# Attention with V stationary and the turned probabilities split and moving

## The reference, cut to what matters

```python
def one_block(qb):
    s = jnp.einsum('bqhd,bkhd->bhqk', qb, k, preferred_element_type=jnp.float32) * scale
    p = jax.nn.softmax(s, axis=-1)
    return jnp.einsum('bhqk,bkhd->bqhd', p.astype(v.dtype), v)
```

## Time and profile before

| | us |
|---|---|
| median of 3 timed runs | 3041.29 |
| lowest and highest | 3038.35, 3042.91 |
| span of the profiled execution | 3038.7 |
| PE busy in it | 2967.0 (98%) |
| DVE, ACT, POOL busy | 1924.1, 1176.6, 1527.5 |
| first score product to first product of the output projection | 120.5 to 641.1 |

### The profile page before, as it was taken

The page is one execution under the profiler, slowest core; times in us unless marked ns, Lnnn a source line. Parts: engine busy times, 40 slices in busy tenths (PEclk is TensorE's granted clock), DMA queues, the critical chain, the costliest instruction groups (busy, mean ns, idle before and its releaser), DMA issues.

```text
span 3038.7 us, 50018 instructions
## 1 busy us (share of the span) xinstructions
PE 2967.0 (98%) x19166; PEld 2684.5 (88%) x19166; DVE 1924.1 (63%) x2960; ACT 1176.6 (39%) x2027; POOL 1527.5 (50%) x997
## 2 busy tenths in 40 slices
PE   8999999999999999999999999999999999999998
PEld 8999999999999999999999988677777788888776
DVE  6677777755534445777788851677778934445666
ACT  4465666641333334553111122232323533334552
POOL 4100000043777777765444444467674577777774
PEclk9999999999999999999999999999999999999998
DMA  3000100021223334442233423333333232235442
GB/s 128 26 30 27 37 26 16 16 100 49 72 95 99 103 100 163 140 144 71 87 117 94 138 90 118 116 119 101 123 94 118 67 107 102 99 103 171 149 130 90
DMA packets 195934, 286.73 MB, mean 94 GB/s; under 512 B 14709, under 2 KB 105077, under 8 KB 195701
## 3 DMA queue, kind: packets, MB, share of 16 engines
q1 hardware_dynamic: 156096, 236.23, 23.8%
q10 hardware_dynamic: 39605, 47.34, 4.7%
HBM read 208.64 MB, written 74.86 MB: 93 GB/s over the span
## 4 chain that ended last, share of the span: by engine, by line
PE 80%; DVE 7%; POOL 5%; issue 4%; DMA 2%; ACT 1%; SPq 1%; DVEq 0%; ACTq 0%; POOLq 0%
PE PS L1272 72%; PE PS L1528 4%; PE PS L1513 2%; DMA Wraw<-in_w 1%; POOL Wlo L1108 1%; POOL Wlo L1168 1%; PE PS L1872 1%; POOL SQ L1213 1%; SPq L911 0%; DVE GD L3627 0%; POOL RMS L1178 0%; POOL Wraw L1126 0%; POOL Wraw L1124 0%; DVE MX L3007 0%; PE PS L2024 0%
## 5 line engine op out<-in xcount | busy, mean ns | idle before, releaser
L1272 PE MATMUL PS<-Uhi,Whi 128*128 128x352 f32 (+2 forms) x2028 | 512.4, 328 | 16.5 <-DVE Ulo L2799 13.8
L1272 PE MATMUL PS<-Uhi,Wlo 128*128 128x352 f32 (+2 forms) x2028 | 507.3, 326 | 0.0
L1272 PE MATMUL PS<-Ulo,Whi 128*128 128x352 f32 (+2 forms) x2028 | 507.0, 326 | 0.0
L1108 POOL TENSOR_TENSOR Wlo<-Wraw,Whi 128x512 fp32r<-128x512 f32 x242 | 329.8, 1366 | 130.4 <-ACT Whi L2442 127.1
L1272 PEld LDWEIGHTS PS<-Uhi,Whi 128*128 128x128 f32 x2028 | 340.9, 189 | 39.4 <-issue 15.9
L1067 POOL TENSOR_TENSOR Whi<-Wraw,const 128x1024 fp32r<-128x1024 f32 x64 | 159.1, 2486 | 418.4 <-PE PS L1272 403.4
L1272 PEld LDWEIGHTS PS<-Ulo,Whi 128*128 128x128 f32 x2028 | 343.5, 189 | 20.3
L1272 PEld LDWEIGHTS PS<-Uhi,Wlo 128*128 128x128 f32 x2028 | 343.4, 189 | 19.5
L2442 ACT ACTIVATE Whi<-Wraw 128x512 fp32r<-128x512 f32 x242 | 151.3, 629 | 330.7 <-POOL Wraw L1126 133.3
L1156 POOL TENSOR_TENSOR Olo<-H,Ohi 128x1056 fp32r<-128x1056 f32 x5 | 12.1, 2444 | 521.8 <-ACT Ohi L2345 521.8
L1272 PE MATMUL PS<-T,Whi 128*128 128x264 f32 (+1 forms) x1328 | 219.1, 288 | 2.1 <-DVE H L3311 1.9
(11 more groups left out here) (431 smaller groups left out, 7114.4 us busy)
## 6 DMA issues: line engine op xcount, KB each, us to landing
Wraw<-in_w SPq DMA_DIRECT2D x192, 256.0 KB, 3.0
Wraw<-in_w SPq DMA_DIRECT2D x91, 512.0 KB, 3.7
Wraw<-in_w SPq DMA_DIRECT2D x168, 128.0 KB, 2.7
xt<-XTT ACTq DMA_DIRECT2D x20, 640.0 KB, 5.7
opd<-HID SPq DMA_DIRECT2D x40, 264.0 KB, 3.4
T<-opd SPq DMA_DIRECT2D x18, 528.0 KB, 4.3
Ulo<-opd SPq DMA_DIRECT2D x17, 528.0 KB, 4.8
Ulo<-opd SPq DMA_DIRECT2D x17, 512.0 KB, 5.5
```

Source lines behind the costliest of these rows:

```text
L1108: pool.tensor_tensor(f.oplo[j % SLOTS], FIRST_S2 if (p, k) == (0, 6) else f.factors[k], f.ophi[j % SLOTS].bitcast(F32), ALU.subtract).then ...
L1272: ins = pe.matmul(out, lhsT, rhs, start=start, stop=stop, skip_group_check=True)
```

## The change

The output product changes sides. V is stationary, and the turned probabilities move. Both are split: for a head x the tile VH[x % 2] holds in 64 of its 128 columns the highs of V and in the other 64 the lows, so that one pass makes both products, in two halves of the partitions. The turned probabilities of a sequence are collected in PTH (highs) and PTL (lows), [106, 5 key blocks, 528 queries]. A product runs for half a sequence, 264 queries: five key blocks, high and low of the probabilities, ten instructions. The four halves of a head run on PE at the steps 5, 7, 10 and 12 behind the head's first (10 and 12 are n = 0 and 2 of the next head), one step after the step that follows their last operand. The result has features on the partitions. ACT copies the other half of the partitions aside (`other_half`), and DVE adds the two into H (`add_outputs`); both stand one step behind the product. It is not scaled: the sums of a pair are inverted at once (`invert`), transposed, sent through DRAM to all partitions (`save_sums`, `load_sums`) and multiplied in on POOL (`scale_outputs`); for the last pair PE spreads them (`spread_sums`) and DVE multiplies (`scale_last`). `outputs` in float32, `evict`, `take_turned`, `turn_outputs` and `take_outputs_of` go.

The split of the turned probabilities takes all five blocks on ACT (`high_turned`, two instructions a step) and again on DVE (`low_turned`, two). The turn and scaling of queries and keys, all their lows, half of the key highs, the lows of V and of the weights move from DVE and ACT to POOL. The first result of `maximum` goes to an unused column of the score bank in PSUM instead of an SBUF tile.

```diff
+PV_TURNS = {5: (0, 0), 7: (0, 1), 10: (1, 0), 12: (1, 1)}
 # PE, step t
-                if t >= 2:
-                    outputs(t - 2)
+                if half_at_turn(t):
+                    outputs(*half_at_turn(t))
+        def outputs(x, s, h):
+            pe.wait_ge(pt_high, 2 * last_block(x, s, h) + 2)
+            pe.wait_ge(pt_low, 2 * last_block(x, s, h) + 2)
+            pe.wait_ge(v_lo, x + 1)
+            if (x, s, h) != (0, 0, 0):
+                pe.wait_ge(o_evicted, half_number(x, s, h))
+            of = slice(h * QHALF, (h + 1) * QHALF)
             for b in range(KB):
+                low = PTL[b // TURN_FIRST][:, b % TURN_FIRST, of]
+                for i, probs in enumerate((PTH[:, b, of], low)):
+                    ins = mm(PS[:, A_OUT, 0:QHALF], VH[x % 2][:, s * KB + b, :], probs,
+                             start=(b == 0 and i == 0), stop=(b == KB - 1 and i == 1))
 # ACT, step t
-                    take_turned(t - 1)
-                if t >= 0:
-                    exponentials_of(t)
-                if t >= 2:
-                    evict(t - 2)
+                    high_turned(t - 1)
+                exponentials_of(t)
+                if half_at_turn(t, 1):
+                    other_half(*half_at_turn(t, 1))
+                if j and j % 4 == 0 and n == 1:
+                    high_values(j)
                 if nxt < HEADS:
-                    if n == 5:
+                    if n == 3 and nxt % 4:
+                        high_values(nxt)
+                    if n == 6:
                         high_q(nxt)
-                    if n == (1 if nxt % 2 else 6):
+                    if n == 7 and nxt % 2 == 0:
                         high_k(nxt)
 # DVE, step t
-                if t >= 0:
-                    maximum(t)
+                maximum(t)
                 if t >= 1:
-                    take_turned(t - 1)
-                    invert(t - 1)
+                    low_turned(t - 1)
+                if half_at_turn(t, 1):
+                    add_outputs(*half_at_turn(t, 1))
+                if j and j % 2 == 0 and n == 1:
+                    invert(j // 2 - 1)
                 if nxt < HEADS:
                     if nxt % 2 == 0 and n < 2:
                         key_factors(nxt // 2, n)
-                    if n == (0 if nxt % 2 else 5):
-                        scale_keys(nxt)
-                    if n == 4:
-                        turn_queries(nxt)
-                    if n == (7 if nxt % 2 else 6):
-                        low_q(nxt)
-                    if n == (2 if nxt % 2 else 7):
-                        low_k(nxt)
-                    if n in ((6, 9) if nxt % 2 else (8, 9)):
+                    if n in (8, 9):
                         query_factors(nxt, n == 9)
+        def add_outputs(x, s, h):
+            own, n = slice(x % 2 * VD, (x % 2 + 1) * VD), half_number(x, s, h)
+            vec.wait_ge(ob_made, n + 1)
 # POOL, head j
+            if nxt % 2:
+                scale_keys(nxt)
+            if j and j % 4 == 0:
+                low_values(j)
+            if nxt % 2:
+                high_k(nxt)
+                low_k(nxt)
+            if nxt % 4:
+                low_values(nxt)
+            if j % 2 and split_unit(j) is not None:
+                low_weights(j)
+            if j >= 4 and j % 2 == 0:
+                scale_outputs(j // 2 - 2)
+            turn_queries(nxt)
+            if j % 2 == 0 and split_unit(j) is not None:
+                low_weights(j)
+            if nxt % 2 == 0:
+                scale_keys(nxt)
+            low_q(nxt)
+            if nxt % 2 == 0:
+                low_k(nxt)
 # maximum, DVE
-            step(vec.tensor_reduce(MX[:, t % RING:t % RING + 1], PS[0:CW, score_bank(t):score_bank(t) + 2, 0:QHALF], AX_XY, ALU.max))
+            most = PS[0:CW, score_bank(t), QHALF:QHALF + 1]
+            step(vec.tensor_reduce(most, PS[0:CW, score_bank(t):score_bank(t) + 2, 0:QHALF], AX_XY, ALU.max))
```

More of the change, by code:

```diff
@@ L389, in prep_orders @@
             stats.append(("t", nxt // 2))
+        elif j:
+            stats.append(("s", j // 2 - 1))
         stats.append(("q", nxt))
-        if turned_pair(j) is not None:
-            prep += [("o", turned_pair(j), s) for s in both]
         if nxt % 4 == 0:
@@ L407, in score_bank, with half_at_turn, half_number, sums_slot @@
     n = t - (HEADS - 1) * PER_HEAD
-    return A_PREP if n in (1, 3, 5, 7) else A_SCORE
+    return A_PREP if n > 0 and n % 2 else A_SCORE
+PV_TURNS = {5: (0, 0), 7: (0, 1), 10: (1, 0), 12: (1, 1)}
+def half_at_turn(t, late=0):
+    for n, (s, h) in PV_TURNS.items():
+        x, rest = divmod(t - late - n, PER_HEAD)
+        if rest == 0 and 0 <= x < HEADS:
+            return x, s, h
+    return None
+def half_number(x, s, h):
+    return 4 * x + 2 * s + h
+def sums_slot(x):
+    return K_R1SQ if x % 2 else (K_R1, K_RB)[x // 2 % 2]
+def last_block(x, s, h):
+    return x * PER_HEAD + s * KB + (KB - 1 if h else KB // 2)
 def split_unit(j):
@@ new lines, in high_k, with low_k, low_values @@
+        def high_k(x):
+            pool.wait_ge(k_scaled, 2 * x)
+            pool.tensor_tensor(KHI[x % 2][:], KSC[x % 2], one.broadcast_to([P, T]), ALU.mult).then_inc(k_hi, 1)
+        def low_k(x):
+            pool.wait_ge(k_hi, x + 1)
+            pool.tensor_tensor(KLO[x % 2][:], KSC[x % 2], KHI[x % 2][:].bitcast(F32), ALU.subtract).then_inc(k_lo, 1)
+        def low_values(x):
+            own, other_ = (slice(e * VD, (e + 1) * VD) for e in (x % 2, 1 - x % 2))
+            pool.wait_ge(v_hi, x + 1)
+            pool.tensor_tensor(VH[x % 2][:, :, other_], V[:, :, x // 2 % 2, own], VH[x % 2][:, :, own].bitcast(F32),
+                               ALU.subtract).then_inc(v_lo, 1)
@@ L1583, in _ @@
                         query_norms(nxt, n - 4)
-                    o = 4 if nxt % 2 else 6
-                    if turned_pair(j) is not None and o <= n < o + 2:
-                        turn_outputs(turned_pair(j), n - o)
                     if nxt % 4 == 0 and n >= 6:
@@ L1593, in _ @@
                             key_norms((nxt + 1) // 2, n - 8)
-                elif n == 8:
-                    turn_outputs(PAIRS - 1, 0)
         t = HEADS * PER_HEAD
         turn_probs(t - 1)
-        outputs(t - 2)
-        outputs(t - 1)
-        turn_outputs(PAIRS - 1, 1)
+        pe.wait_ge(stats_taken, len(STATS))
+        pe.wait_ge(p_full, t)
+        spread_sums(0)
+        for h in range(2):
+            outputs(HEADS - 1, 1, h)
+        spread_sums(1)
         now["slot"] = None
@@ L2385, in _ @@
         t = HEADS * PER_HEAD
-        take_turned(t - 1)
-        evict(t - 2)
-        evict(t - 1)
-        take_outputs_of(PAIRS - 1, 1)
+        high_turned(t - 1)
+        for h in range(2):
+            other_half(HEADS - 1, 1, h)
         high_out(PAIRS - 1)
```

362 lines of the change are left out of this document (208 added, 154 removed).

## The result

The changed kernel takes 3185.29 us (median of 4 runs, 3174.65 to 3199.14), the one before 3040.72 in the same comparison: 1.0477 of the time, 95% interval 1.0441 to 1.0512. The forecast was 3083 us with a range up to 3112; the sign was right, the size was not: +145 us instead of +42.

The account below looks back on a forecast made before the run. The prediction took a 2.95 us loop through scores, maximum, factor and exponential to bound light steps. Steps +12, POOL +20, ends +5 and clock +5 made +42 us: 3083 us, range 3062 to 3112.

Parts of the forecast that it names:

- a loop of 2.95 us: Attention steps: scores, maximum, factor, exponential, then the next scores into the same PSUM bank; a step costs at least 2.95 us.
- the 2.9 that was to mean a shorter loop: Sign of being wrong: light attention steps under 2.9 us would mean the loop got shorter.
- PE is the bound: Rival: PE's work sets the attention stage's time, so the change gains 92 us, 2949 us; faster in all had chance 0.16.
- The step table: Times of a head's ten steps from PE work, loop and queue delays: four heads 135.5 against 132.5, +12 us over 15.
- the forecast's 4.9 for POOL: Second part of the query factors waits for POOL's key high and low; the next maximum is 4.9 us late.
- +5, between 0 and 20 if light steps n = 8 and 9 suffice: Clock term: the four stalls lower PE's granted clock towards 1.2 GHz, costing 5 us in all.
- the four stalls of GpSimd: Ends of heads j = 1, 5, 9, 13, where POOL's key operations hold VectorE's query factors, about 5 us each.
- the fall in the light steps of each head: Rival: clock falls there, or POOL's chain comes too late: 2 us more per head, above 3112 us; chance 0.06.
- a half above 1.3 us: Sign of being wrong: half products costing PE more than 1.3 us each, where 1.21 was forecast.
- the term said 20: POOL term: VectorE's query factors held at four places, 4.9 us each, +20 us in all.
- The ends: Start, last head and tail: +1 for the start, +2 for the last head, +2 at the end, together +5 us.
- The maximum in PSUM: Maximum's first result in PSUM instead of SBUF: plus or minus 8 us over 160 steps, taken as nothing.

Follow-up runs that it names:

- e9: The kernel before the change, output products cut to the first of five in every step (1,280 of 1,600 left out): 3053.3 us, 1.0038.
- e7: e6 with the unread products of e1 added: 3090.9 us, 1.0164.
- e1: The changed kernel plus unread products of 248 columns behind the turns of light steps (4, 6, 8, 9): 3149.5 us, 1.0350.
- e6: The changed kernel, first query-factor instruction moved to step 6 and GpSimd's key scaling of odd heads held back: 3147.7 us, 1.0345.
- e11: The changed kernel with only GpSimd's key scaling of odd heads held until the previous head's query factors are made: 3167.4 us, 1.0418.
- e13: e6 with halves at steps 4, 6, 9, 1, unread products in 5, 7, 8, and the query factors' whole first part at step 6: 3054.1 us, 1.0040.
- e12: e13 with the maximum kept in SBUF in place of PSUM: 3052.7 us, 1.0032.
- e3: The changed kernel with e1's unread products and the query factors moved to steps 6 and 9 or 6 and 7: 3133.4 us, 1.0296.

## Why the prediction was wrong in size

- **The bound.** Right: a loop of 2.95 us holds the light steps (2.87 to 2.96 after; 2.87 is just below the 2.9 that was to mean a shorter loop), and PE's relief of 9.0 to 4.85 us a head buys almost nothing. The rival "PE is the bound" (2949 us) fell at the first row: step 1 at 2.94 with less work. e9 shows it a second time: less work, not less time.
- **The step table.** Right at full clock: step 5 3.38 to 3.40 (forecast 3.30), step 4 3.68 (3.48), step 7 of an even head 4.75 (4.40), step 9 behind the factors 4.00 (3.95). e7, which has the clock and lacks the two waits, takes 140.69 for four heads, the forecast's 140.4. That agreement is partly luck: the forecast's 4.9 for POOL are not in it, and the steps are 5.2 longer in their place, above all at step 9 of head 7 (5.75 against 4.04), at step 6 of head 4 (4.43 against 2.95) and in the steps 4 (3.68 against 3.48). At step 9 of head 7 PE waits 1.39 us for VectorE's copy of V, which stands behind the query factors; the forecast counted only the maximum behind them, and the kernel before already took 4.93 us there.
- **The clock.** This is the step that failed first. The prediction charged "+5, between 0 and 20 if light steps n = 8 and 9 suffice", for what follows the four stalls of GpSimd, and gave 0.06 to the fall in the light steps of each head. The unread products alone bring back 36 us (e1), and 57 when the waits are gone (e6 to e7). The row was at hand: 0.57 in the window behind the tail, after products of 64 and 106 columns with gaps of 0.4 to 0.6 us. The step table itself gave PE 1.2 to 2.16 us of work in most of the steps of 2.95, so pauses of a quarter and more of a step, and the table was then worked out with every product at the full clock. One of the prediction's own signs of being wrong was a half above 1.3 us: at the low clock it took 2.35.
- **The norms.** Not in the forecast at all. It listed what stands on VectorE behind the add and when the next maximum would start; it didn't ask who waits for the first operation of the factors. PE does, for 2.9 or 3.3 us at step 8 of every even head but the last. Step 8 was put at 3.15 and took 5.72 to 6.42. This wait was never taken away alone; e6 less e11 puts it at 20 us.
- **GpSimd.** The mechanism is right, the place is not. By the forecast the key scaling passes before the second part of the factors, which then waits for the high and the low of the keys, 4.9 us, once in four heads. Its own times said otherwise: the first part ends 4.95 us from the start of step 8, that is 2.0 us into step 9, and the key scaling begins at 1.05. So the first part is hit, and in both odd heads, while the forecast put the meeting of head 7 at no cost. In head 5 it lengthens step 9 by 3.8 us over the 3.95 forecast, and the second part is held for 0.5. e11 gives 18 us for taking the meeting away alone, where the term said 20. That closeness is luck: seven meetings that cost less, partly taken back at the low clock, stand for four of 4.9.
- **The ends.** Last head and tail +10.6 instead of +4; in e13 +3.5 (650.19 - 618.98 against 27.72). So two thirds of it go with the clock and the order of e13; the runs don't separate the two.
- **The maximum in PSUM.** Nothing, as taken: -1.4 us between e13 and e12.

Put together: 3185 less 95 us for the waits and the clock is e7's 3091. That is 8 us over the forecast, but the forecast had 20 and 5 us for just these two; held against 3058, without them, e7 is 33 us over. The step table explains 19 or 20 of it (5.2 in four heads), falls of the clock that the unread products didn't prevent another 11 or 12 (heads 1, 2, 3, 10, 11 and 12 are that much longer than their like among heads 4 to 7). What isn't settled: why the same steps let the clock fall in one head and not in another (in e9, steps 6 and 7 take 3.74 and 3.71 us in head 5 and 2.95 in head 9, with the same instructions); and whether a form with these halves can beat the kernel before. e12, the nearest, is 0.3% behind, and its unread products had no real work put in their place.

## What to carry to other kernels

Before you count what a lighter engine saves, look at what it does in its pauses: if TensorE's work falls below a loop that other engines set, the saved time is a pause, and a pause can cost you the clock for the heaviest step that comes next. Price the heavy steps at both clock levels when a change thins out the light ones. And when an instruction moves behind another in one queue, list who waits for its semaphore, not only what stands behind it.

## What the runs showed of the hardware

- The kernel ran faster with more for TensorE to do: six to ten unread products of 248 columns in up to four steps of a head took 36 to 57 us off (e1, e7); 1,280 products less added 12 us to the kernel before (e9: granted clock 0.86 in the heads, 1.00 before). In e9 the clock fell (at 379.14) with no gap of TensorE above 0.5 us in the steps before it (0.47 and 0.48 in the rows), and with ten products of one column in the last of them.
- VectorE and GpSimd exclude each other at operations as small as ten columns between SBUF operands: 1.75, 1.80 and 2.32 us instead of 0.17, each until GpSimd's operation ended. With a PSUM operand they don't (0.72 at 370.67), and, what I hadn't expected, neither does the operation of one column: 0.21 to 0.22 inside a GpSimd operation and outside (e12). The Trainium skill, SBUF — State Buffer, "SBUF: two separate sides", ties the lock to two SBUF inputs or a two-port mode of VectorE. The trace agrees for the operations with two SBUF inputs (2.32 us in e3); the one at 366.10 has one SBUF input and is held for 1.75 us, and no run here shows in which mode it ran.
